# First attention of the two-block layer: tiles of 8 rows by 16 columns against 12 by 32 keys, two heads at a time, with the projections reordered and the convolution's taps moved forward

## The reference

```python
hx = modulate(rms_norm(x, norm1_g[i]), sh1, sc1)
hc = modulate(rms_norm(ctx, norm1_g[i]), csh1, csc1)
qx, kx, vx, ux = split_proj(hx @ w_in[i])          # 512 + 512 + 512 + 1024 features
kvc = hc @ w_in[i][:, ATT_DIM:3 * ATT_DIM]         # keys and values of 256 context tokens
qx_rot = axial_rope(qx, row_pos, col_pos); kx_rot = axial_rope(kx, row_pos, col_pos)
attn_x = neighbourhood_attention(qx_rot, qx, kx_rot, vx, kc, vc, rpb[i])
conv_x = conformer_conv(ux, dw_kernel[i], dw_bias[i], conv_ln_g[i], conv_ln_b[i])
x_new = x + g1 * (jnp.concatenate([attn_x, conv_x], axis=-1) @ w_out[i])
```

## Time and profile before

| what | us |
|---|---|
| median of 3 runs (2840.02 to 2843.12) | 2840.64 |
| profiled execution, whole | 2845.75 |
| its span | 2843.8 |
| PE busy | 2695.1 |
| DVE busy | 1400.0 |
| POOL busy | 941.3 |
| ACT busy | 722.3 |

### The profile page before, as it was taken

The page is one execution under the profiler, slowest core; times in us unless marked ns, Lnnn a source line. Parts: engine busy times, 40 slices in busy tenths (PEclk is TensorE's granted clock), DMA queues, the critical chain, the costliest instruction groups (busy, mean ns, idle before and its releaser), DMA issues.

```text
span 2843.8 us, 34883 instructions
## 1 busy us (share of the span) xinstructions
PE 2695.1 (95%) x14056; PEld 2177.4 (77%) x14056; DVE 1400.0 (49%) x1526; ACT 722.3 (25%) x1004; POOL 941.3 (33%) x443
## 2 busy tenths in 40 slices
PE   6999799998899999999989989999999999989899
PEld 3888577776688888888867757887888878778777
DVE  3635888874454445444447668883003221352331
ACT  4200133333221111111114436662000020141010
POOL 1334522201344443444433310004434434523333
PEclk8999799999899999999999999999999999999999
DMA  5111222212111111111121100001111111112112
GB/s 238 38 38 53 70 77 77 62 65 82 44 38 52 47 49 52 44 52 44 52 89 45 45 16 1 1 1 45 48 63 45 52 45 45 67 38 104 45 38 89
DMA packets 36674, 155.88 MB, mean 55 GB/s; under 512 B 4164, under 2 KB 4296, under 8 KB 35016
## 3 DMA queue, kind: packets, MB, share of 16 engines
q1 hardware_dynamic: 33264, 127.04, 13.1%
q10 hardware_dynamic: 1528, 20.71, 1.8%
q0 software_dynamic: 1760, 6.36, 0.9%
HBM read 145.70 MB, written 8.39 MB: 54 GB/s over the span
## 4 chain that ended last, share of the span: by engine, by line
PE 84%; DVE 10%; issue 2%; DMA 2%; ACT 1%; POOL 1%; DVEq 0%; ACTq 0%; POOLq 0%
PE region L265 22%; PE region L267 22%; PE region L266 22%; PE pv L696 4%; DVE conv L820 3%; PE region L796 2%; PE aux L684 2%; PE aux L1399 2%; PE pv L342 1%; PE region L798 1%; DVE prob L1480 1%; DVE tmp L418 1%; DMA x_sb<-x_t 1%; PE pv L506 1%; DVE h_lo L412 1%
## 5 line engine op out<-in xcount | busy, mean ns | idle before, releaser
L1772 POOL TENSOR_TENSOR w_hi<-w_raw,der 128x1024 fp32r<-128x1024 f32 x186 | 360.1, 1936 | 1662.4 <-PE region L267 1616.7
L265 PE MATMUL region<-h_hi,w_hi 128*128 128x512 f32 x1760 | 694.0, 394 | 43.8 <-DVE h_lo L412 20.6
L266 PE MATMUL region<-h_lo,w_hi 128*128 128x512 f32 x1760 | 690.0, 392 | 0.0
L267 PE MATMUL region<-h_hi,w_lo 128*128 128x512 f32 x1760 | 689.6, 392 | 0.0
L1775 POOL TENSOR_TENSOR w_lo<-w_raw,w_hi 128x1024 fp32r<-128x1024 f32 x186 | 500.0, 2688 | 14.6
L265 PEld LDWEIGHTS region<-h_hi,w_hi 128*128 128x128 f32 x1760 | 333.7, 190 | 123.2 <-issue 48.8
L267 PEld LDWEIGHTS region<-h_hi,w_lo 128*128 128x128 f32 x1760 | 333.4, 189 | 70.0
L266 PEld LDWEIGHTS region<-h_lo,w_hi 128*128 128x128 f32 x1760 | 333.8, 190 | 68.5
L265 PE MATMUL region<-ff_hi,w_hi 128*128 128x512 f32 x512 | 199.2, 389 | 0.0
L266 PE MATMUL region<-ff_lo,w_hi 128*128 128x512 f32 x512 | 199.2, 389 | 0.0
L267 PE MATMUL region<-ff_hi,w_lo 128*128 128x512 f32 x512 | 199.2, 389 | 0.0
(11 more groups left out here) (323 smaller groups left out, 4269.3 us busy)
## 6 DMA issues: line engine op xcount, KB each, us to landing
w_raw<-units SPq DMA_DIRECT2D x186, 512.0 KB, 3.6
w_raw<-w_ada_late SPq DMA_DIRECT2D x32, 512.0 KB, 3.6
ada_buf<-w_ada SPq DMA_DIRECT2D x4, 2048.0 KB, 14.1
toep<-rpb_pad POOLq DMA_DIRECT2D x16, 288.0 KB, 5.6
x_sb<-x_t ACTq DMA_DIRECT2D x2, 2048.0 KB, 14.0
x<-x_t ACTq DMA_DIRECT2D x1, 4096.0 KB, 13.0
x_spill<-x ACTq DMA_DIRECT2D x1, 4096.0 KB, 11.8
x<-x_spill ACTq DMA_DIRECT2D x1, 4096.0 KB, 14.3
```

The source lines that it names most:

```text
L265: pe.matmul(dst, wh, xh, start=first, stop=False)
L266: pe.matmul(dst, wh, xl, start=False, stop=False)
L267: return pe.matmul(dst, wl, xh, start=False, stop=last)
L1772: pool.tensor_tensor(w_hi[:, s], w_raw[:, s], one_col.broadcast_to([P, 1024]), ALU.mult)\
```

## The change

- The units come as u, k, v, q. `EARLY_TAPS` is gone: `proj1_dve` runs 10 taps after each of the four u pairs, 4 after each k, 7 after each v and 2 after each q, 92 of the 124.
- The transposed values are copied by ACT into `v_out`, written to memory (`v_spill`) and read back in pieces (`v_pair`, 16 transfers per pair of heads, 512 bytes per packet), arranged by column block. q is written by ACT in tile order, and the last addition of its rotation on DVE writes it in tile order.
- A tile is now 128 queries (8 rows by 16 columns) of two heads: 32 tiles. Per head there are 384 window keys (12 rows by 32 columns) and 256 context keys, 640 in all. The two heads' score products use rows 0 to 63 and 64 to 127 of PE and are issued alternately; the two heads' value products write partitions 0 to 63 and 64 to 127 of `pv`, also alternately, with the values as weights. The output has features on partitions, so `turn_back` is gone; ACT and DVE split it per tile (`hi`, `lo`) into `mixa_hi` and `mixa_lo`.
- The probabilities are divided by their sum on DVE before they are transposed (`norm`).
- The bias comes ready from memory: 24 transfers of 384 KB on SP's queue. POOL builds none.
- A piece of the late modulation is computed in each tile; its 32 results are added at the end in one instruction.
- No `meet` stands between projections and attention.

The core of the diff:

```diff
-STAGE_UNITS = [("q", 4), ("k", 4), ("v", 4), ("u", 8), ("out1", 8), ("mlp", 16 * FF_GROUPS), ("lat", 6),
+STAGE_UNITS = [("u", 8), ("k", 4), ("v", 4), ("q", 4), ("out1", 8), ("mlp", 16 * FF_GROUPS), ("lat", 6),
...
     def proj1_dve(e, pos, ch):
...
-            if j < 3:
-                for n in range(EARLY_TAPS * j, EARLY_TAPS * (j + 1)):
-                    conv_tap(e, ch, n)
+            some_taps(10)
...
+            e.tensor_tensor(k_rot[:, j], k_rot[:, j], tmp[:, 0], ALU.add).then_inc(sem("rope_done"), 1)
+            reach(e, "rope_done", j + 1)
+            some_taps(4)
+        for j in range(4):
+            pos.next_use(), pos.next_use()
+            if j:
+                v_ctx_dve(e, j - 1)
+            some_taps(7)
...
+            for rb in range(2):
+                last = e.tensor_tensor(by_tile(q_rot[j], rb), by_row(src, rb), by_row(tmp[:, 0], rb), ALU.add)
...
+            some_taps(2)
+        return taps
...
+    NA_N = HEADS // 2 * TT
+
+    def na_pe(e, pos):
...
+            for s in range(2):
+                wait_region(e, uses[s])
+            late_pe(e, i)
+            if i:
+                late_turn_pe(e, i - 1)
+            for s in range(2):
+                e.matmul(region[:, s, 0:CTX], q_t[rows[s], j, q], k_ctx[rows[s], j], start=True, stop=True)
+            for lo, n in ((0, 8), (8, 4)):
+                for s in range(2):
+                    at = CTX + lo * K_COLS
+                    last = e.matmul(region[:, s, at:at + n * K_COLS].rearrange("p (r c) -> p r c", c=K_COLS),
+                                    q_rot[j][rows[s], q], keys[rows[s], lo:lo + n], start=True, stop=True)
+                    if lo:
+                        last.then_inc(sem("na_scored"), 1)
...
+        def values(i):
...
+            reach(e, "na_pt_act", 2 * i + 2)
+            reach(e, "na_pt_dve", i + 1)
+            if i:
+                reach(e, "na_lo", i)
...
+            for b in range(NKT):
+                for s in range(2):
+                    d = slice(64 * s, 64 * s + 64)
+                    v = v_ctx[:, b, j * P + 64 * s:j * P + 64 * s + 64] if b < 2 else v_pair[j % 2][:, cb, rb + b - 2, d]
+                    last = e.matmul(pv[d, 0, 0:P], v, na_prob_t[:, i % 2, s, b], start=(b == 0), stop=(b == NKT - 1))
...
+        for i in range(NA_N + 3):
+            if i < NA_N:
+                scores(i)
+            if 2 <= i < NA_N + 2:
+                turn(i - 2)
+            if i >= 3:
+                values(i - 3)
...
+    def na_dve(e, pos, ch, taps):
+        def most(i, s):
...
+            if s:
+                e.sem_inc(free[s], 1)
+            else:
+                late_dve(e, i)
+                e.sem_inc(free[s], 1)
...
+        for i in range(NA_N + 4):
+            if i < NA_N:
+                most(i, 0)
+                most(i, 1)
+            if 2 <= i < NA_N + 2:
+                move(i - 2)
+            if i >= 4:
+                lo(i - 4)
+            if 1 <= i < NA_N + 1:
+                norm(i - 1)
+            for n in left[len(left) * i // NA_N:len(left) * (i + 1) // NA_N]:
+                conv_tap(e, ch, n)
...
-            turn_back_act(act, pos, "nt", mix_hi)
...
-            turn_back_dve(dve, pos, "nt", mix_hi, mix_lo)
...
-            turn_back_pe(pe, pos, "nt", o_tok)
```

More of the change, by code:

```diff
@@ L637, in proj1_dve, with some_taps @@
+    def proj1_dve(e, pos, ch):
+        taps = iter(range(N_TAPS))
+        def some_taps(n):
+            for _ in range(n):
+                conv_tap(e, ch, next(taps))
+        e.memset(bias_t[0][:, :, 0:CTX], 0.0).then_inc(sem("bias_zero"), 1)
         for j in range(4):
@@ new lines, in na_act, with hi, move, exps @@
+    def na_act(e, pos, ch):
+        def hi(i):
+            j, q = divmod(i, TT)
+            reach(e, "na_summed", 2 * i + 2)
+            copy(e, na_out(mixa_hi, j, q), pv[:, 0, 0:P].rearrange("p (r n) -> p r n", n=Q_COLS))\
+                .then_inc(sem("na_hi"), 1)
+        def move(i, s):
+            reach(e, "na_turned", 3 * i + 1 + s)
+            if i >= 2:
+                reach(e, "na_summed", 2 * (i - 1))
+            copy(e, na_prob_t[:, i % 2, s, 0:4], aux[:, s * HALF:(s + 1) * HALF].rearrange("p (b k) -> p b k", k=P))\
+                .then_inc(sem("na_pt_act"), 1)
+        def exps(i, s):
+            c = 2 * (i % 4) + s
+            reach(e, "na_shift", 2 * i + s + 1)
+            p = na_prob[:, i % 3, s]
+            e.activation(p, p, ACT.Exp, bias=na_neg[:, c:c + 1], accum_out=na_sum[:, c:c + 1])\
+                .then_inc(sem("na_exp"), 1)
+        for i in range(NA_N + 4):
+            if i >= 4:
+                hi(i - 4)
+            for s in range(2):
+                if 2 <= i < NA_N + 2:
+                    move(i - 2, s)
+                if i < NA_N:
+                    exps(i, s)
+        pos.use += 2 * NA_N
@@ new lines, in v_pair_load, with bias_load @@
+    def v_pair_load(e, j):
+        for cs, first in enumerate(FIRST_COL):
+            for r in range(4):
+                src = v_spill[j].rearrange("(g r c) f -> r c g f", r=4, c=W_GRID)[r, first:first + K_COLS]
+                e.dma_start(v_pair[j % 2][r * K_COLS:(r + 1) * K_COLS, cs], src).then_inc(sem(f"v_pair_ld{j % 2}"), 16)
+    def bias_load(e, n):
+        if n >= 4:
+            reach(e, "na_most", 2 * max(i for i in range(NA_N) if bias_of(i) == n - 4) + 2)
+        e.dma_start(bias_t[n % 4][:, :, CTX:], na_bias[n]).then_inc(sem(f"bias_ld{n % 4}"), 16)
@@ L1975, in _ @@
             tell()
-            ended(5)
+            ended(4)
             mla_pe(pe, pos)
```

479 lines of the change are left out of this document (255 added, 224 removed).

## The result

The changed kernel takes 2764.86 us (median of 4 runs, 2761.63 to 2767.49), the kernel before beside it 2841.88 (4 runs): a ratio of 0.973 (95% interval 0.972 to 0.975), 77 us less. The forecast was 2760. The span of the profiled execution is 2761.0 us against 2843.8.

The account below looks back on a forecast made before the run. PE bound the attention before; afterwards a loop through PE and DVE would. Attention -76, projections +2.6 and layer norm -7.5 gave -81: 2765 on the profiled execution, 2760 by the median. Forecast's own range 2745 to 2780, full range 2722 to 2808.

Parts of the forecast that it names:

- The tile: Attention: PE and DVE wait for each other in each tile, 6.7 us per tile, 31 periods 207 us.
- DVE alone: Rival in the attention: DVE's own 5.7 us sets the tile, 31 x 1.0 us less, 2729; chance 0.12.
- The heads' overlap: Attention scores of two heads overlap, 1.3 us; rival without overlap: loop 1.2 us longer, +37, 2797, chance 0.20.
- The start: Attention's start: -4 for three periods without values, +8 for half clock, +3 for transfers ahead of late piece 2.
- The half clock: Attention's start: PE at half clock, its 3.3 us doubling for two or three tiles, +8 us.
- The tail: Attention's end: from the last maximum to the layer norm, the last three tiles passed on, about 14 us.
- Transfers and clock as bounds: Attention rivals: transfers bind, waits of 10 to 20 us, 2775, chance 0.06; PE stays at half clock, +96, 2856, chance 0.07.
- Projections: Up to the first maximum: more DVE taps, slowed by POOL, and waits of PE and DVE, +2.6 us (-13 to +10).
- The price of a split: Projections: each POOL split costs DVE 3.6 us; eighteen splits, +65 us.
- Layer norm: After the attention: without `turn_back` ACT squares earlier and the sums end near 660, -7.5 us; only -2 at half clock.
- Behind it: Output projection and everything after it: untouched, 0 us.
- The sum: Whole kernel: -76 + 2.6 - 7.5 = -81 us on the profiled 2845.75, that is 2765.

Follow-up runs that it names:

- Run 1: Changed kernel with DVE's subtraction `lo` moved ahead of the two maxima and the move in each tile: 2729.16 us.
- Run 3: Changed kernel with all but one of the attention's 32 convolution taps left out: 2765.06 us.
- run 5: Changed kernel with both heads' score products on PE rows 0 to 63, the second head's scores being those of the first: 2797.41 us.
- run 2: Changed kernel with all score products of head 0 issued ahead of those of head 1 instead of alternately: 2761.85 us.
- run 7: Run 1 with v_pair 1 behind late piece 2, and v_pair 1 to 3 each issued as four transfers in each of four tiles: 2714.94 us.
- run 9: Changed kernel with 64 semaphore increments nobody waits for, hidden in PE's 16.7 us wait at the attention's start: 2755.73 us.
- run 6: Changed kernel with 64 semaphore increments nobody waits for added to PE's program just ahead of the MLP's loop: 2761.93 us.

## Why the prediction was right

**The tile.** Predicted 6.7, measured 6.68. The pieces: two maxima with the late copy 2.17 against 2.18, move 0.43 against 0.42, `lo` 0.35 against 0.28, values 1.23 against 1.25 (483.39 to 484.64), late piece 0.79 against 0.88, scores 1.3 against 1.29. Runs 1 and 3 show that it is this loop and neither engine's sum.

**DVE alone.** I had put its work at 5.7 us, it is 5.15. Each form had been taken with its gap, and the taps at 1.32 are 1.28. So this rival lay 1.5 us per tile away, not 1.0. Run 1 brought it about, and that it landed on the rival's 2729 is chance: 1.5 us in each of 31 tiles would have been 2718, and most of the rest are PE's waits for late pieces.

**The heads' overlap.** Right, and its price of 37 us was +33 in run 5. The price depends on the alternate order, in which DVE's first maximum waits for nearly all of the products: in run 2's order 0.54 us more of score products cost nothing.

**The start.** The transfers were put at +3 (0 to 10). I had late piece 2 land 15 us after DVE's first maximum, by its bytes, and wanted after 13. It landed 14.5 us after (348.96), but was wanted after 8.3, when DVE's second maximum of tile 2 (341.83, and the instruction behind it to 342.8) freed the region: so it cost 6.3 of the 8.53 us that PE sat idle. The failed half is the time of need: the first two tiles have no values in them. And though the landing came out by bytes, it was the place in the queue that made it: the 16 small transfers hold SP's queue for 8.39 us, 0.52 each for 64 KB, about as long as one bias of 384 KB (0.55), and run 7 removed the wait by spreading them over the queue, with the bytes unchanged. The half clock was put at +8 for two or three tiles; it lasts to 356 and covers three tiles, and without PE's second wait (run 7) it ended at 339. It comes again only in short stretches. First maximum to first sum came out at 228.9, predicted 228; the three terms of the start were right in their sum only. The tail from the last tile's first maximum (549.16) is 14.2 us, predicted 14.

**Transfers and clock as bounds.** Neither happened: 132 GB/s with no waits in steady tiles, and a granted clock of 0.97 with PE busy for 136 of 190 us. With 1.95 us idle in 6.68 us and 10 transposes per tile the clock held; what the prediction feared of the transposes did not show here.

**Projections.** Predicted +2.6, measured -1.5. The steps that failed are two waits: PE's for `v_ctx` (6 us) and DVE's for the last q did not occur. The price of a split beside DVE was right: from 99.19 to 334.47 DVE took 235.3 us, of which the prediction counts 171.4 as its own, so 64 us for 18 splits, 3.6 each. The trace agrees: DVE's instructions there take 231.1 us, and would take about 166 if each took the shortest time that its form shows.

**Layer norm.** -9.7 against -7.5. Eight of it is `turn_back` (from the deviation's start to the end of the sums 10.85 us instead of 18.9); the rest is the clock: the 16 first sums take 7.13 us at a granted 1.00 and took 8.83 at 0.81.

**Behind it.** The prediction said that all behind the output projection is untouched. The instructions are, but their place in the program is not, and PE's gaps in the MLP's loop, a term that the prediction put at nothing, cost 13.0 us in this profiled execution (9.1 us by run 9's median, of which a part may lie ahead of the loop: its profiled execution reached the output projection 4.4 us earlier). It shows as +3.2 only, because the later stages took 9.8 us less than before. Behind the MLP 58.5 us of this execution went at half clock, 71.7 in the kernel before; 13.2 us fewer at half clock give back 6.6 us at most, and the rest is open. Only run 2's execution was like it (57.4), all others had 70.0 to 71.7, and why is open too. Run 9's takes 2171.6 us from the output projection on, as the kernel before.

**The sum.** The spans of the two profiled executions differ by 82.8 us, predicted 81. The attention, 75 of it, came out by its mechanism. The other terms were off by -4.1 (projections), -2.2 (layer norm) and +3.2 us (behind it), and that they nearly cancel is luck.

## What to carry to other kernels

When two engines wait for each other once per tile and neither is full, draw the loop through both, and ask of each instruction in it whether someone waits for what stands behind it: one 0.28 us subtraction in a better place gave 36 us. Then look at what the faster loop uncovers, queue by queue: a queue that issues small transfers holds up what stands behind them by their number more than by their bytes (here 0.52 us for 64 KB, 0.55 for 384 KB). And after any change of an unrolled stage look at the returns of the loops behind it, for gaps with no releaser; a few instructions that do nothing, put where the engine waits anyway, may be worth more than they cost.

## What was not expected of the hardware

- PE idles 2.2 to 3.4 us at each return of a loop of 1581 instructions that begins, by the compiled program, at 0.82 of a block of 256 instructions, and under 0.3 us where it begins at 0.07.
- 64 semaphore increments take PE 8.8 us, 0.14 each (run 6).
- Score products of two row groups overlap also where they are issued one head after the other: 1.83 us, between 1.29 (alternately) and 2.37 (same rows).
- PE keeps a granted clock of 0.97 while idle for 28% of the time in gaps of 2 us; PE's wait of 16.7 us at the start of the attention went with a clock of 0.50, and so did, for 3.4 us, two of the three gaps of 3 us in the MLP.
